# A ninth place for gathered expert rows in the second layer, and a quarter of the descriptor space

## The reference, cut to what matters

```python
def peer(h, w_q, keys, u, v):           # 8 heads, 128 keys a half, 16 kept: 128 experts a token
    qh = (x @ w_q).reshape(T, PEER_HEADS, 2, PEER_HALF)
    ...
    experts = jnp.take_along_axis(cidx, top_pos, axis=-1)
    gates = jax.nn.softmax(top_s, axis=-1)
    ...
        act = jax.nn.gelu(jnp.einsum('thkd,td->thk', u[eb], xb))
        return jnp.einsum('thk,thkd->td', (gb * act).astype(xb.dtype), v[eb])
```

## Time and profile before

| | us |
|---|---|
| median of 3 runs | 4246.91 |
| lowest and highest of them | 4234.9, 4251.95 |
| the profiled execution, its own time | 4234.23 |
| its span, first to last instruction | 4232.1 |

### The profile page before, as it was taken

The page is one execution under the profiler, slowest core; times in us unless marked ns, Lnnn a source line. Parts: engine busy times, 40 slices in busy tenths (PEclk is TensorE's granted clock), DMA queues, the critical chain, the costliest instruction groups (busy, mean ns, idle before and its releaser), DMA issues.

```text
span 4232.1 us, 32788 instructions
## 1 busy us (share of the span) xinstructions
PE 2981.6 (70%) x9343; PEld 1539.7 (36%) x9343; DVE 3022.8 (71%) x6125; ACT 1425.6 (34%) x4133; POOL 1623.8 (38%) x1311
## 2 busy tenths in 40 slices
PE   4699766876777645757778776868775887555565
PEld 1365352454433202423463233543453633212221
DVE  0406779978988666787669868769786787666666
ACT  1213323522233313246423333523552233322232
POOL 0001332434544434344334434435343345544554
PEclk8798887988989866878889988879887998897888
DMA  8243897989999997999899989999999999999998
GB/s 321 91 162 134 334 405 270 343 343 368 405 367 415 407 413 313 387 387 408 357 359 372 401 361 366 374 365 400 383 371 369 357 416 403 422 421 418 404 421 371
DMA packets 222323, 1521.91 MB, mean 360 GB/s; under 512 B 29758, under 2 KB 33538, under 8 KB 48823
## 3 DMA queue, kind: packets, MB, share of 16 engines
q0 software_dynamic: 187200, 1370.25, 80.6%
q1 hardware_dynamic: 34942, 149.58, 9.0%
HBM read 1516.49 MB, written 3.24 MB: 359 GB/s over the span
## 4 chain that ended last, share of the span: by engine, by line
DMA 31%; PE 30%; DVE 23%; issue 7%; ACT 4%; POOL 3%; DVEq 1%; SPq 1%; PEldq 1%; PEld 0%; ACTq 0%; POOLq 0%
DMA core_ring<-in_l_uv,core_experts 26%; PE sum_rows L1946 8%; DVE core_ring L1906 6%; DVE core_yv L1921 4%; POOL core_ring L1889 3%; PE sum_rows L2213 2%; PE j_in_ps L471 2%; PE j_query_pq L1679 1%; PE s1c_query_pq L1679 1%; PE s1b_in_ps L471 1%; DMA s0a_h_w<-in_l_peer_wq 1%; DMA mod_w<-in_l_w_mod 1%; DMA s1b_h_w<-in_l_peer_wq 1%; PE s0b_out_po L610 1%; DVEq L158 1%
## 5 line engine op out<-in xcount | busy, mean ns | idle before, releaser
L1889 POOL DMA_INDIRECT core_ring<-in_l_uv,core_experts x1280 | 1609.0, 1257 | 2259.7 <-PE sum_rows L1946 1081.4
L1946 PE MATMUL sum_rows<-core_ring,core_diag 128*128 128x512 f32 x3100 | 1681.3, 689 | 670.5 <-ACT core_diag L1935 540.3
L1906 DVE CUSTOM_DVE_ANT_0 core_ring<-core_ring,core_hc 128x1024 f32<-128x1024 f32 x1280 | 1551.8, 1223 | 723.6 <-DMA core_ring<-in_l_uv,core_experts 487.1
L1946 PEld LDWEIGHTS sum_rows<-core_ring,core_diag 128*128 128x128 f32 x3100 | 631.4, 217 | 1643.6 <-ACT core_diag L1935 897.0
L1929 ACT ACTIVATE core_wt<-core_wt 128x1 f32<-128x1 f32 x1280 | 256.5, 200 | 1675.0 <-DVE core_wt L1906 1583.3
L1921 DVE SCALAR_TENSOR_TENSOR core_yv<-core_ring,core_wt,core_yv 128x1024 f32<-128x1024 f32 x495 | 634.0, 1281 | 13.3 <-ACT core_wt L1932 12.8
L1932 ACT ACTIVATE core_wt<-core_wt,core_gates 128x1 f32<-128x1 f32 x1280 | 376.8, 294 | 41.6
L1935 ACT ACTIVATE core_diag<-core_ident,core_wt 128x128 f32<-128x128 f32 x775 | 311.2, 401 | 25.3
L2213 PE MATMUL sum_rows<-core_ring 128*128 128x416 f32 x320 | 118.4, 530 | 5.2 <-DVEq L158 4.1
L1929 ACT ACT_TABLE_LOAD x81 | 103.9, 1283 | 5.2 <-DVEq L158 3.8
L1906 DVE DVE_READ_ACCUMULATOR2_ANT core_wt<- 128x1 f32 x1280 | 104.9, 82 | 0.0
(11 more groups left out here) (772 smaller groups left out, 3055.7 us busy)
## 6 DMA issues: line engine op xcount, KB each, us to landing
mod_w<-in_l_w_mod SPq DMA_DIRECT2D x16, 2048.0 KB, 13.1
core_ring<-in_l_uv,core_experts POOLq DMA_INDIRECT x1280, 10.1
core_ring<-in_l_w_mod POOLq DMA_DIRECT2D x8, 2048.0 KB, 10.9
p_in_w<-in_l_w_in SPq DMA_DIRECT2D x5, 1664.0 KB, 8.9
core_ring<-in_l_w_in POOLq DMA_DIRECT2D x5, 1664.0 KB, 10.6
p_h_w<-in_l_peer_wq SPq DMA_DIRECT2D x16, 512.0 KB, 4.5
s0a_h_w<-in_l_peer_wq SPq DMA_DIRECT2D x16, 512.0 KB, 12.5
s0b_h_w<-in_l_peer_wq SPq DMA_DIRECT2D x16, 512.0 KB, 8.3
```

The source lines that it names most:

```text
L1889: nc.gpsimd.indirect_dma_start(self.ring[:, r, :], None, core.a[f"l{layer}_uv"], bass.IndirectOffsetOnAxis(ap=self.experts[:, t, n:n + 1], ...
L1906: nc.vector.tensor_tensor_reduce(self.ring[:, r, 0:D], self.ring[:, r, 0:D], self.hc[:], 1.0, 0.0, ALU.mult, ALU.add, self.wt[:, r:r + 1]) ...
L1946: mm = nc.tensor.matmul(self.py[:, c * 512:(c + 1) * 512], self.diag[:, r, :], self.ring[:, r, D + c * 512:D + (c + 1) * 512], start=(at = ...
```

## The change

`RINGS = (8, 9)` gives layer 1 nine places. Eight are the places of the ring as before. The ninth is a tensor of its own, `layer1_slot8`, with its own diagonal matrix `layer1_diag8`; both are allocated in a new outer stage `layer1`, which opens after the last stage of layer 0's part has given its memory back. `place(n)` says which place a row has and in which round: n % 8 in layer 0, (n - 640) % 9 in layer 1. Every step of a row asks `place` for its buffer and its semaphores. Which engine sums a row still goes by n % 8. `gather_all` becomes `gather(layer)`, called once for each layer. The descriptor strip falls from 4096 to 1024 bytes of each partition.

```diff
-        self.wt = mem.sb("wt", [P, RING])
+        self.wt = mem.sb("wt", [P, max(RINGS)])
...
-        self.used = [new(f"used{r}") for r in range(RING)]
+        self.used = [new(f"used{r}") for r in range(max(RINGS))]
+        self.slots = [self.ring[:, r, :] for r in range(RING)]
+        self.diags = [self.diag[:, r, :] for r in range(RING)]
...
+    def more_slots(self, stage):
+        for r in range(RING, RINGS[1]):
+            self.slots.append(stage.sb(f"slot{r}", [P, 2 * D])[:])
+            self.diags.append(stage.sb(f"diag{r}", [P, P])[:])
+
+    def place(self, n):
+        half = TILES * SLOTS
+        if n < half:
+            return n % RINGS[0], n // RINGS[0]
+        rnd, r = divmod(n - half, RINGS[1])
+        return r, rnd + (half // RINGS[0] if r < RINGS[0] else 0)
+
     def wait_used(self, eng, n):
-        rnd, r = divmod(n, RING)
+        r, rnd = self.place(n)
         eng.wait_ge(self.used[r], rnd + 2)
...
-                    rnd, r = divmod(q * SLOTS + n, RING)
+                    r, rnd = self.place(q * SLOTS + n)
                     pool.wait_ge(self.used[r], rnd + 1)
-                    nc.gpsimd.indirect_dma_start(self.ring[:, r, :], None, core.a[f"l{layer}_uv"],
+                    nc.gpsimd.indirect_dma_start(self.slots[r], None, core.a[f"l{layer}_uv"],
...
-            bg.gather_all()
+            bg.gather(0)
...
+        with Stage(core, "layer1") as last:
+            bg.more_slots(last)
+            bg.gather(1)
+            with Stage(core, "s1_att") as m:
...
-    nc = _bacc.Bacc("TRN2", target_bir_lowering=False, num_devices=1, dynamic_dma_scratch_size=4096)
+    nc = _bacc.Bacc("TRN2", target_bir_lowering=False, num_devices=1, dynamic_dma_scratch_size=1024)
```

More of the change, by code:

```diff
@@ L1855, in __init__ @@
         self.gelu_done, self.wt_done, self.diag_done = new("gelu_done"), new("wt_done"), new("diag_done")
-        self.used = [new(f"used{r}") for r in range(RING)]
+        self.used = [new(f"used{r}") for r in range(max(RINGS))]
+        self.slots = [self.ring[:, r, :] for r in range(RING)]
+        self.diags = [self.diag[:, r, :] for r in range(RING)]
         self.order = new("order")
         self.gate_in = new("gate_in")
-        self.row_in = [new(f"row_in{r}") for r in range(RING)]
+        self.row_in = [new(f"row_in{r}") for r in range(max(RINGS))]
         self.owners, self.on_pe, self.last_add = [], places_on_pe(4), None
@@ L1879, in _ @@
         def _(pool):
-            for q, (layer, t) in enumerate(self.sequence):
+            for q in range(layer * TILES, (layer + 1) * TILES):
+                t = self.sequence[q][1]
                 pool.wait_ge(self.selected, q + 1)
@@ L1903, in dot @@
         nc = self.core.nc
-        rnd, r = divmod(n, RING)
+        r, rnd = self.place(n)
         dve.wait_ge(self.row_in[r], rnd * 16 + 16)
-        nc.vector.tensor_tensor_reduce(self.ring[:, r, 0:D], self.ring[:, r, 0:D], self.hc[:], 1.0, 0.0, ALU.mult, ALU.add,
+        nc.vector.tensor_tensor_reduce(self.slots[r][:, 0:D], self.slots[r][:, 0:D], self.hc[:], 1.0, 0.0, ALU.mult, ALU.add,
                                        self.wt[:, r:r + 1]).then_inc(self.dot_done, 1)
@@ L1911, in add_row @@
         nc = self.core.nc
-        r = n % RING
+        r, _ = self.place(n)
         dve.wait_ge(self.wt_done, n + 1)
@@ L1926, in weigh @@
         nc = self.core.nc
-        r, t = n % RING, self.sequence[n // SLOTS][1]
+        r, t = self.place(n)[0], self.sequence[n // SLOTS][1]
         act.wait_ge(self.dot_done, n + 1)
@@ L1934, in weigh @@
             act.wait_ge(self.wt_done, n + 1)
-            nc.scalar.activation(self.diag[:, r, :], self.core.env["ident"][:], ACT.Copy, scale=self.wt[:, r:r + 1]
+            nc.scalar.activation(self.diags[r], self.core.env["ident"][:], ACT.Copy, scale=self.wt[:, r:r + 1]
                                  ).then_inc(self.diag_done, 1)
@@ L1940, in sum_rows @@
         nc = self.core.nc
-        r, (q, at) = n % RING, divmod(n, SLOTS)
+        r, (q, at) = self.place(n)[0], divmod(n, SLOTS)
         if at == 0 and q:
@@ L1945, in sum_rows @@
         for c in range(2):
-            mm = nc.tensor.matmul(self.py[:, c * 512:(c + 1) * 512], self.diag[:, r, :],
-                                  self.ring[:, r, D + c * 512:D + (c + 1) * 512], start=(at == 0), stop=(at == SLOTS - 1),
+            mm = nc.tensor.matmul(self.py[:, c * 512:(c + 1) * 512], self.diags[r],
+                                  self.slots[r][:, D + c * 512:D + (c + 1) * 512], start=(at == 0), stop=(at == SLOTS - 1),
                                   skip_group_check=True)
@@ L1970, in _ @@
         def _(dve):
-            for r in range(RING):
+            for r in range(max(RINGS)):
                 dve.sem_inc(self.used[r], 1)
@@ L2414, in program @@
             modulation_stage(core, 1, "mod1", m.sb("silu", [P, DK, 32])[:], early.MOD_CHUNKS, [1, 4], 2, (2.5, PE_0, 3))
[L2415 to L2442, removed]
```

45 lines of the change are left out of this document (35 added, 10 removed).

## The result

The changed kernel takes 4216.0 us (median of 12 runs, 4203.56 to 4227.35) where the kernel before took 4250.07 us in the runs beside it (12 runs, 4234.9 to 4260.77). The ratio of their times is 0.9929, with a 95% interval of 0.9914 to 0.9943: 30 us or 0.7% faster, between 24 and 37.

The account below looks back on a forecast made before the run. Took the middle stretch to lose time when DMA engines run dry and DVE then waits for rows, the last to be transfer-bound. Ninth place -26 us, all else 0: 4208.2 us profiled, 4221 us measured; range 4203 to 4262.

Parts of the forecast that it names:

- middle stretch: 2406 to 3570 us, where layer 1's rows run behind stages in front; DMA share forecast to go from 0.94 to about 0.96.
- The ninth place, -26 us: Middle stretch: 15 dry spells of the DMA engines, 29.0 us together, less three small ones; DVE's row waits to some 90.
- the price of one row for a spell: One row's transfer, 2.49 us: the most by which a ninth place shortens each dry spell of the DMA engines.
- the first spell: Beginning of layer 1, window from 2420 us with DMA share 0.79: counted as a full spell, 2.5 us.
- the upper end: Largest gain allowed: 29.0 us of dry spells plus about 2 us at the change of tiles after 3900 us, making 31.
- Gather 648 near 2422 us: Start of layer 1: sign that the forecast is right, gather 648 issued near 2422 instead of 2434 us.
- Last stretch, 0: From 3570 us to the end, only rows: transfers keep the DMA engines busy, so earlier queueing gains 0.
- Layer 0 and the new streams' ends, 0: Up to 2406 us, same places and semaphores: 0; one POOL branch and one DVE semaphore increment: under 1 us.
- The smaller strip, 0: POOL's descriptor strip, 1024 bytes holding 7 gathers: cost taken as 0, since 2.1 rows under way keep the engines busy.
- Rival 1, hidden anyway: Middle stretch is paced by stages, so other waits replace row waits: gain 0 to 10 us, 4237 to 4247; chance 0.32.
- Rival 2, the weights: An extra queued row delays weight loads PE awaits, up to 2.49 us each: 20 us slower, 4267; chance 0.10.
- Rival 3, the strip emptied each time: Both layers: POOL empties its queue every seventh gather, shown by landing-long gathers or gaps: +340 us, 4587; chance 0.08.

Follow-up runs that it names:

- experiment 3: Changed kernel with nine places for rows 640 to 1023 only, eight for the last two tiles: 4212.15 us, ratio 0.9926 to the kernel before.
- experiment 4: Changed kernel with eight places up to row 1023, nine for the last two tiles only: 4244.38 us, ratio 0.9999 to the kernel before.
- experiment 2: Changed kernel with seven places in layer 1 instead of nine, strip 1024 bytes: 4342.27 us, ratio 1.0234 to the kernel before.
- experiment 1: Kernel before with a descriptor strip of 1024 instead of 4096 bytes, eight places throughout: 4246.8 us, ratio 1.0015 to the kernel before.
- experiment 11: Kernel before with a strip of 1024 bytes and 3072 bytes kept free so buffers keep their addresses: 4245.19 us, ratio 1.0009 to the kernel before.
- experiment 6: Changed kernel with a descriptor strip of 2048 instead of 1024 bytes: 4201.41 us, ratio 0.9907 to the kernel before.
- experiment 7: Changed kernel with a descriptor strip of 1536 instead of 1024 bytes: 4206.5 us, ratio 0.9918 to the kernel before.
- experiment 8: Changed kernel, strip 1024 bytes, with 1024 bytes kept free so buffers lie as with a 2048-byte strip: 4210.11 us, ratio 0.9922 to the kernel before.
- experiment 5: Changed kernel with a descriptor strip of 512 instead of 1024 bytes, nine places: 4450.0 us, ratio 1.0483 to the kernel before.
- experiment 9: Changed kernel with eleven places from row 905 on, strip 1024 bytes: 4204.86 us, ratio 0.9915 to the kernel before.

## Why the prediction was right, step by step

*Where the gain lies: shown.* The forecast was a gain in the middle stretch alone, and experiments 3 and 4 put it there.

*The ninth place, -26 us: right in kind, and near in size partly by luck.* The middle stretch got 31 us shorter, the times 30. The share went to 0.96 as forecast, two windows show the price of one row for a spell (+0.10), and DVE's waits for rows fell to 77 us, not to some 90. But the sum took a spell's dry time for time won, spell by spell, and that did not hold:

- The dry time itself fell by 20 us, not 26. The small spells from 2645 to 2745 us and those from 2970 to 3170 gave some 14 of the 17 us counted for them. The spells around `s1b_in` and `s1c_query` and the one at 3495, 7 us of the count, gave nothing.
- The two attention stages won 24 us, more than the 17 us of spells counted in or beside them; the first spell, the price of which reads so clearly, stands in a part that won 5 us at most.
- The rest of the 31 us is time in which the engines were busy, and the sum has no term for it. The gathers' packets in the middle stretch, before and now (queue, packets, MB, share of 16 engines):

```profile
q0 software_dynamic: 55927, 406.27, 87.2%
...
q0 software_dynamic: 55948, 406.34, 88.7%
```

That is 1015 us of 1164 before and 1005 of 1133 now, for the same bytes. All five profiles with eight places in this stretch have 1012 to 1015 us, the five with nine 1003 to 1007 (406 to 408 MB in each). Why the same rows take the engines less time is not shown.

So too much was counted in some stages and too little in others, and the two errors nearly cancel. With a strip that holds more, the stretch was 38 to 43 us shorter than the earlier trace rows, beyond the 31 of the upper end.

*Gather 648 near 2422 us.* It went out 17.5 us after gather 640, for 16.2 forecast; the layer itself began 10.4 us later in this execution.

*Last stretch, 0.* 662 us both times, and 0.9999 with the ninth place there alone; some 3 us may lie there by the profiles (experiment 4). I had the reason, transfers, but not how near it was: with seven places it breaks (experiment 2).

*Layer 0 and the new streams' ends, 0.* The first stretch's 10 us stand against 6.8 of scatter in before alone, so the 0 is not contradicted, and not shown either.

*The smaller strip, 0: nearly.* Experiments 1 and 11 bound it at -2 to 11 us with eight places, and 6 to 8 suggest some 5 to 12 with nine. The reason I gave was partly wrong: I had 2.1 rows as what must be under way, and with three the kernel loses 235 us. That 1024 bytes hold seven, as worked out from the 16 B of the Trainium skill's page "DMA: Bandwidth & Descriptors", section "Terms", was right: experiments 5, 8 and 9 show 3 and 7 as the most under way. One reading was wrong without weight: the packets beside the gathers' are not 20 equal loads but 27 transfers of several sizes.

*Rival 1, hidden anyway: no for the whole.* Some 9 of 40 us came back as other waits, mostly for PE. Around `s1b_in` and `s1c_query` it fits: no time was won there.

*Rival 2, the weights: a trace of it.* `s1b_query` waits 15.6 us as before, `s1b_in` 10.6 for 8.8, all of PE's waits for weights rose by 5.6 us, and the chain has a load between the parts of `s1b_in` now. DVE's waits for rows fell by 40.

*Rival 3, the strip emptied each time: no.* POOL waits for one landing, even with room for three gathers. The sign named for it, gathers as long as a landing, would have missed a full strip: it shows as runs of 0.9 and 1.56 us.

The 4221 us were 5 too many: the gain was 4 us larger than forecast.

## What to carry over

A buffer more in a ring is worth about one transfer for a spell in which the DMA engines run dry and the consumer waits behind it. Counting spells in short windows gave the size here (26 us for 30), but not the places: 24 of 31 us came in the two attention stages, and next to nothing around the projections `s1b_in`, `s1c_out` and `s1c_query`. So compare the lengths of stages, not of windows. Where transfers bind it is worth next to nothing, but only as long as the places cover the time from a place's gather to its release divided by the time of one transfer; here 7.8 by estimate, and eight held where seven cost 64 us. The descriptor strip is a ring of its own: keep it larger than the gathers that have to be under way, and read runs of POOL's equal pairs of idle and instruction time, at the pace of transfers, as the sign that it is full.

## What the runs showed of the hardware

A full strip shows no wait of its own in the trace. It appears as "issue" ahead of a gather and as a longer gather, several in a row: 0.9 and 1.56 us for 0.30 and 0.94.

A DMA share of 1.00 does not mean the full rate: with three gathers under way the window read 1.00 at 398 GB/s, with seven 1.01 at 421.
